# The byte places of matmul operands in a fp32r transformer layer: activations and slabs 128 bytes past the weight ring, one temporary in PSUM

## The chip, the core and the metric

The kernel runs on one core of one Trainium2 chip. The metric is the device time of one execution in microseconds. Before the change the median of three runs is 1975.04 us (1974.83 to 1975.86). A measurement is one launch; the profile is of one execution of its own.

## What is computed

One layer of a decoder: 512 tokens, width 2048, all in float32. A combined input projection feeds four mixers (pooling, convolution, two sparse attentions), then comes an output projection, a normalisation, a SwiGLU block and a second normalisation:

```python
D_MODEL, SEQ, DEPTH = 2048, 512, 1
D_FF = 5632
mix = jnp.concatenate([y_pool, y_conv, y_dsa, y_nsa], axis=-1)
x = _layernorm(DN_ALPHA * x + mix @ w_out[l], ln1_g[l], ln1_b[l])
gate, up = jnp.split(x @ w_gate_up[l], 2, axis=-1)
x = _layernorm(DN_ALPHA * x + (jax.nn.silu(gate) * up) @ w_down[l], ln2_g[l], ln2_b[l])
```

The part that the change is about is the last two lines, the feed-forward block, 1206 of the 1973 us of the span.

## The kernel before

**Three matmuls for one.** Every float32 operand is split into a high part (a cast to fp32r) and a low part (the operand less its high part). A product takes three fp32r matmuls: high by high, high by low, low by high. In the code a group of three lines is one such step: L795 to L797, L1030 to L1032, L1148 to L1152, L1197 to L1201, L1237 to L1239. Each `matmul` call is a load of 128 weight columns (the second argument, the stationary operand) and a matmul that streams the third argument, the moving operand. ScalarE makes the high parts (L1485), VectorE the low parts (L2034).

**The feed-forward block** is cut by a scheme of seven block products in place of eight (`PIECES = 7`). It runs in 62 units, one behind the other. 42 are chunks (`chunk`): 128 hidden features of gate and up, 7 products of 24 matmuls with 256 moving columns. In a chunk the ring of weight granules is the weights; what moves is `act` in products 1, 5, 6 and 7, and the block sums in `x_room` (products 2 and 3) and in `xs_4` (product 4, shown as `xs`). 20 are down units (`down`), two after every third chunk of four: 7 products of 12 matmuls with 512 moving columns. There the ring granule moves, and the weights are blocks of the hidden values: `h01` and `h23` (shown as `h`), `hs21` and `hs4` (shown as `hs`). After the last chunk a tail of 16 blocks of 12 long matmuls finishes the down product, on granules in `w_room` and, for every second pair, in `x_room` (`late`).

**Earlier products.** The input projection uses whole slabs in `w_hi` and `w_lo` (L795). The output projection (L1030) has `act` as weights and a slab as moving operand; the slab lies in `w_room` or, for a part, in `x_room`. The first gate and up slabs use `w_room` and `xs_4`.

**Places in SBUF.** Tensors stand one behind the other in a partition. `w_room` starts at byte 2240, 192 modulo 512. Ring granules are slices of it at multiples of 4096 bytes (`ring_hi`), or that plus 512 (`ring_lo`), so they are at 192. Slabs start `SHIFT` columns later: with `SHIFT = 8`, 32 bytes, at 224. `act`, `raw` and all tensors of the feed-forward stage up to `x_room` start at 224. Slabs and block sums in `x_room` start `SHIFT` columns into it, at 256; `xs_4` is at 256. The late granules start at the front of `x_room`, at 224. Columns of a slice step by multiples of 512 bytes, so a slice has its tensor's place.

**Order of work around the change.** Each engine's order is written out by hand and the engines meet at counting semaphores. In a chunk ScalarE copies intermediate sums out of PSUM, takes SiLU of the first half (L1579, `p5_temp`) and of the second (L1585, `g2_temp`); VectorE multiplies (L2134, h2). `g2_ready` and `h2_ready` count these. `temps` holds five temporaries of 256 columns, `g2_temp` the first. In a down unit ScalarE copies the first product, `d1` (banks 2 and 3), into `d2` (banks 0 and 1) at L1597, and TensorE's third product accumulates there behind `down_seeded`. PSUM banks 4 and 5 hold `r1`, bank 6 `r2`, bank 7 `r3`, each in its first 256 columns.

Of the kernel before, what the change touches and what calls it, by code (L numbers as in the profile page):

```python
# [21 lines left out]
F32 = mybir.dt.float32  # L22
F32R = mybir.dt.float32r
ALU = mybir.AluOpType
ACT = mybir.ActivationFunctionType
AX = mybir.AxisListType

P = 128
SEQ = 512
# [34 lines left out]
FF_CHUNKS = D_FF // P  # L64
# [34 lines left out]


GRAN = SLAB // 2
SHIFT = 8
HALF_TOKS = SEQ // 2
S_ORDER = ("s1", "s2", "s4", "s3")
TAIL_SLOTS = ((0, 32), (2, 32), (4, 63), (5, 63), (1, 32), (3, 32), (0, 33), (2, 33))
# [36 lines left out]
def build(nc, x, x_t, w_in, w_out, pool_w, pool_scale, conv_w, conv_b, conv_ln_g, conv_ln_b, conv_pw_w,  # L142
          conv_pw_b, cmp_pos_k, cmp_pos_v, cmp_k_w1, cmp_k_w2, cmp_v_w1, cmp_v_w2, ln1_g, ln1_b,
          ln2_g, ln2_b, w_gate_up, w_down, out):
    with ExitStack() as ctx:
        def sb(name, shape, dt=F32, where=ctx):
            return where.enter_context(nc.sbuf_tensor(name, shape, dt))
# [12 lines left out]
        act_hi, act_lo = act[:, 0, :, :], act[:, 1, :, :]  # L160
        raw = sb("raw", [P, 2, SLAB])

        mixing = ExitStack()
        with mixing:
            def sbm(name, shape):
# [34 lines left out]
        hs21 = sb("hs21", [P, 2, 2, SEQ], F32R, feed)  # L200
        stage = sb("stage", [P, 4, 2, SEQ], F32, feed)
        raw_c = sb("raw_c", [P, 2, GRAN], F32, feed)
        temps = sb("temps", [P, 5, HALF_TOKS], F32, feed)
        a12_scope = ExitStack()
        with a12_scope:
            a12 = sb("a12", [P, KT // 2, HALF_TOKS], F32, a12_scope)
# [80 lines left out]
                     "s3": act_lo[:, 0:kh, HALF_TOKS:SEQ]}  # L287
        s_source = {"s1": s1, "s2": a22, "s4": a12, "s3": a11}

        g2_temp, s_temp, p5_temp, p16_temp, p167_temp = (temps[:, i, :] for i in range(5))  # L290
        rstd_diagonal, ones_row = temps[:, 0, 0:P], temps[0:1, 0, P:2 * P]
        feed_ident, small = temps[:, 1, 0:P], temps[:, 1, P:2 * P]
        stats = small[:, 0:TT * 24].rearrange("p (i n s) -> p i n s", i=TT, n=4)
        moments = small[:, TT * 24:TT * 26].rearrange("p (i s) -> p i s", i=TT)
        rstd, shift = small[:, TT * 26:TT * 27], small[:, TT * 27:TT * 28]
        silu_g = temps[:, 3:5, :].rearrange("p a n -> p (a n)")
        r1 = [psum[:, 4 + i, 0:HALF_TOKS] for i in range(2)]
        r2, r3 = psum[:, 6, 0:HALF_TOKS], psum[:, 7, 0:HALF_TOKS]
        d1, d2, d3 = psum[:, 2:4, :], psum[:, 0:2, :], psum[:, 5:8:2, :]
# [492 lines left out]
        def _(pe):  # L792
# [457 lines left out]
            for e in range(16):  # L1250
                i, n = e // 4, e % 4
                if e < 2:
                    pe.wait_ge(x21_copied, N_DOWN)
                elif e < 4:
                    pe.wait_ge(x11_copied, N_DOWN)
                elif e >= 8:
                    pe.wait_ge(tile_added, added + e - 8 + 1)
                elif e == 4:
                    pe.wait_ge(c11_done, FF_CHUNKS - 2)
                    pe.wait_ge(g2_ready, FF_CHUNKS - 2)  # L1260
                    pe.wait_ge(c12_done, FF_CHUNKS - 1)
                for k in range(4):
                    piece = 2 * n + k // 2
                    if e == 0 and k == 0:
                        pe.wait_ge(hid_lo, hid_last - 2)
                    if k == 3 and n == 0 and i in (0, 2):
                        pe.wait_ge(hid_lo, hid_last - 1 + i // 2)
                    if i == 0 and piece < 4:
                        pe.wait_ge(lo_ready, TAIL_Q + piece + 1)
                    elif i == 0:  # L1270
                        pe.wait_ge(late_low, piece - 3)
                    w_h, w_l = late[piece - 4] if piece >= 4 else (ring_hi(TAIL_Q + piece), ring_lo(TAIL_Q + piece))
                    mm = down_products(i, k, e % 8, w_h, w_l, k % 2)
                mm.then_inc(tail_tile, 1)
# [16 lines left out]
        def _(act):  # L1291
# [232 lines left out]
            def chunk(un):  # L1524
                m, par, g = un.m, un.par, un.m // 4
                j, prev, kind = m % 2, (m - 1) % 2, m % 4
                last = g == FF_GROUPS - 1

                act.wait_ge(gran_done, un.q + 1)
                if m == 0:  # L1530
                    act.wait_ge(silu_done, 2)
                else:
                    act.wait_ge(g2_ready, m)
                nc.scalar.copy(r2, r1[par]).then_inc(p1_seeded, 1)
                unit_high(un, 4)
                if kind in (1, 2):
                    act.wait_ge(h2_ready, m)
                    part_high(h22, prev, p167_temp)
                elif m > 0:
                    act.wait_ge(h2_ready, m)  # L1540
                    part_high(h11, prev, nat[:, prev, 0:HALF_TOKS])

                act.wait_ge(gran_done, un.q + 2)
                if m > 0:
                    act.wait_ge(h1_ready, m)
                nc.scalar.copy(p5_temp, r3).then_inc(p5_copied, 1)
                unit_high(un, 5)
                if kind in (1, 2) and not last:
                    act.wait_ge(base_stored[1], 16)
                    act.wait_ge(s_nat, 6 * g + 2 * kind + 1)  # L1550
                    part_high(hs21, prev, nat[:, prev, :])
                    act.wait_ge(s_nat, 6 * g + 2 * kind + 2)
                    part_high(hs4, prev, s_temp)
                elif kind == 3 and g == FF_GROUPS - 2 or kind == 0 and last:
                    part_high(hs3, prev, nat[:, prev, HALF_TOKS:SEQ])
                elif kind in (0, 3) and m > 0:
                    act.wait_ge(s_nat, 6 * (g + (1 if kind == 3 else 0)) + prev + 1)
                    part_high(hs3, prev, s_temp)

                act.wait_ge(gran_done, un.q + 3)  # L1560
                if m == 0:
                    act.wait_ge(hid_ready, 2)
                elif kind in (1, 2):
                    act.wait_ge(hid_lo, low_count(m - 1, "a12"))
                nc.scalar.copy(p16_temp, r2).then_inc(p16_copied, 1)
                unit_high(un, 6)

                act.wait_ge(gran_done, un.q + 4)
                following(un, 0)

                act.wait_ge(gran_done, un.q + 5)
                if kind in (1, 2):
                    act.wait_ge(hid_lo, low_count(m - 1, "a22"))
                nc.scalar.copy(p167_temp, r2).then_inc(p167_copied, 1)
                following(un, 1)

                act.wait_ge(gran_done, un.q + 6)
                act.wait_ge(c22_ready, m + 1)
                nc.scalar.activation(p5_temp, r1[par], ACT.Silu).then_inc(c11_done, 1)  # L1579
                following(un, 2)  # L1580

                act.wait_ge(gran_done, un.q + 7)
                if m > 0:
                    act.wait_ge(h2_ready, m)
                nc.scalar.activation(g2_temp, r2, ACT.Silu).then_inc(g2_ready, 1)  # L1585
                if kind in (0, 1):
                    act.wait_ge(h1_ready, m + 1)
                    part_high(h12, j, p16_temp)
                following(un, 3)

            def down(un):
# [2 lines left out]
                act.wait_ge(gran_done, un.q + 1)  # L1594
                if k > 0:
                    act.wait_ge(x21_copied, k)
                nc.scalar.copy(d2, d1).then_inc(down_seeded, 1)  # L1597
                unit_high(un, 4)

# [88 lines left out]
        def _(ve):  # L1688
# [388 lines left out]
            def chunk(un):  # L2077
# [53 lines left out]
                ve.wait_ge(g2_ready, m + 1)  # L2131
                ve.wait_ge(c22_ready, m + 1)
                h2 = p167_temp if kind < 2 else nat[:, j, HALF_TOKS:SEQ]
                nc.vector.tensor_tensor(h2, p167_temp, g2_temp, ALU.mult).then_inc(h2_ready, 1)  # L2134

            def down(un):
                k = un.k
# [116 lines left out]
```

## Time and profile before

| | |
|---|---|
| median of 3 runs | 1975.04 us |
| profiled execution | 1974.57 us |
| its span | 1972.8 us |
| TensorE matmul, weight load | 1963.5 us, 1732.0 us |
| VectorE, ScalarE, GpSimd | 1412.7, 848.8, 504.1 us |
| DMA | 264.28 MB, mean 134 GB/s |

The span runs from the first to the last instruction; 1.8 us of the execution lie around it. Busy time of TensorE counts overlapping matmuls once and their ends are modelled, so the mean duration of a matmul in the profile (280 ns for 256 moving columns) is longer than the spacing at which they start. The spacing is read from a stretch that holds one kind alone, as its length over the count of matmuls in it. The counts (x98 and the like) that a view of stretches gives take in matmuls that run across an edge, one to three more than start in it; a product of a chunk is 24 matmuls, one of a down unit 12. The granted clock was the full one, 2.4 GHz, over the whole span (PEclk 9 is 90% or more; the profile gives a mean of 1.0).

### The profile page before, as it was taken

Reading aid. Unit: us, or ns where it says so; the run is one execution under the profiler, and the core shown is the slowest. Engines: PE = TensorE matmul, PEld = TensorE weight load, DVE = VectorE, ACT = ScalarE, POOL = GpSimd, SP = SyncE. Lnnn points to the kernel's source line nnn. Section 1 sums busy time; section 2 is a strip of 40 time slices with the busy share of each in tenths; the row PEclk is TensorE's granted clock in tenths of the full one; section 3 lists DMA queues with packets and bytes.
Section 4 is the critical chain, followed back from the end, with each engine's and each line's share of the span. In section 5 each row is a group of like instructions: output and inputs, shape, how many; then the busy total and the mean of one; then the engine's idle time right before and its main releaser. Section 6 shows DMA issues by size and latency. Waiting matters only on the chain.

```text
span 1972.8 us, 30224 instructions
## 1 busy us (share of the span) xinstructions
PE 1963.5 (100%) x12301; PEld 1732.0 (88%) x12301; DVE 1412.7 (72%) x1911; ACT 848.8 (43%) x1280; POOL 504.1 (26%) x343
## 2 busy tenths in 40 slices
PE   9999999999999999999999999999999999999999
PEld 7777888766888999998989999898998989999897
DVE  3079997263112988787878888788788878878776
ACT  3011000364000645555555555555555555555553
POOL 2555656244557310202011020201102020110200
PEclk9999999999999999999999999999999999999999
DMA  7433343500534433938466494755739376493972
GB/s 213 106 87 85 86 106 85 176 22 22 213 102 133 150 84 113 193 103 182 118 148 152 128 176 125 156 144 120 180 107 192 113 156 150 110 197 91 198 248 87
DMA packets 316429, 264.28 MB, mean 134 GB/s; under 512 B 12262, under 2 KB 258854, under 8 KB 313482
## 3 DMA queue, kind: packets, MB, share of 16 engines
q1 hardware_dynamic: 292026, 211.97, 37.4%
q0 software_dynamic: 23616, 46.15, 14.2%
q10 hardware_dynamic: 656, 4.33, 0.6%
q8 instruction: 93, 1.52, 0.3%
q14 instruction: 38, 0.31, 0.1%
HBM read 211.95 MB, written 50.33 MB: 133 GB/s over the span
## 4 chain that ended last, share of the span: by engine, by line
PE 98%; DVE 1%; DMA 1%; SPq 0%; ACT 0%; issue 0%; DVEq 0%
PE psum L1148 14%; PE psum L1150 14%; PE psum L1152 14%; PE psum L795 7%; PE psum L797 7%; PE psum L796 7%; PE psum L1199 7%; PE psum L1201 7%; PE psum L1197 7%; PE psum L1030 3%; PE psum L1031 3%; PE psum L1032 3%; PE psum L1009 1%; PE psum L946 1%; PE psum L937 1%; PE psum L997 1%
## 5 line engine op out<-in xcount | busy, mean ns | idle before, releaser
L2034 DVE TENSOR_TENSOR w_room<-raw,w_room 128x1024 fp32r<-128x1024 f32 x310 | 379.3, 1223 | 157.2 <-ACT w_room L1485 157.1
L1485 ACT CAST w_room<-raw 128x1024 fp32r<-128x1024 f32 x312 | 328.7, 1053 | 209.6 <-DVE raw L2045 67.0
L765 POOL DMA_DIRECT2D out<-stage x160 | 139.5, 1471 | 1028.4 <-DVE stage L2145 1007.6
L1148 PE MATMUL psum<-act,w_room 128*128 128x256 f32 x1344 | 375.8, 280 | 0.0
L1150 PE MATMUL psum<-act,w_room 128*128 128x256 f32 x1344 | 375.5, 279 | 0.0
L1152 PE MATMUL psum<-act,w_room 128*128 128x256 f32 x1344 | 375.3, 279 | 0.0
L1148 PEld LDWEIGHTS psum<-act,w_room 128*128 128x128 f32 x1344 | 252.7, 188 | 0.5
L1150 PEld LDWEIGHTS psum<-act,w_room 128*128 128x128 f32 x1344 | 252.6, 188 | 0.5
L1152 PEld LDWEIGHTS psum<-act,w_room 128*128 128x128 f32 x1344 | 252.8, 188 | 0.0
L795 PE MATMUL psum<-act,w_room 128*128 128x512 f32 (+2 forms) x608 | 232.0, 382 | 1.6 <-DVE act L1709 1.6
L797 PE MATMUL psum<-act,w_room 128*128 128x512 f32 (+2 forms) x608 | 229.9, 378 | 0.0
L796 PE MATMUL psum<-act,w_room 128*128 128x512 f32 (+2 forms) x608 | 229.9, 378 | 0.0
L673 POOL TENSOR_TENSOR w_room<-raw,w_room 128x2048 fp32r<-128x2048 f32 (+1 forms) x45 | 207.5, 4612 | 3.7
L2034 DVE TENSOR_TENSOR w_room<-raw_c,w_room 128x1024 fp32r<-128x1024 f32 x124 | 151.5, 1222 | 59.0 <-ACT w_room L1485 57.2
L1148 PE MATMUL psum<-x_room,w_room 128*128 128x256 f32 x672 | 185.6, 276 | 0.0
L1152 PE MATMUL psum<-x_room,w_room 128*128 128x256 f32 x672 | 185.5, 276 | 0.0
L1150 PE MATMUL psum<-x_room,w_room 128*128 128x256 f32 x672 | 185.5, 276 | 0.0
L670 POOL TENSOR_SCALAR w_room<-raw 128x2048 fp32r<-128x2048 f32 (+1 forms) x45 | 88.8, 1973 | 259.7 <-PE psum L797 136.6
L795 PEld LDWEIGHTS psum<-act,w_room 128*128 128x128 f32 (+1 forms) x608 | 113.8, 187 | 27.3 <-issue 5.1
L797 PEld LDWEIGHTS psum<-act,w_room 128*128 128x128 f32 (+1 forms) x608 | 113.8, 187 | 22.1
L796 PEld LDWEIGHTS psum<-act,w_room 128*128 128x128 f32 (+1 forms) x608 | 113.8, 187 | 22.0 <-issue 0.5
L1485 ACT CAST w_room<-raw_c 128x1024 fp32r<-128x1024 f32 x126 | 132.7, 1053 | 0.0
(303 smaller groups left out, 4131.9 us busy)
## 6 DMA issues: line engine op xcount, KB each, us to landing
raw_c<-in_w_gate_up SPq DMA_DIRECT2D x84, 512.0 KB, 6.6
raw<-in_w_gate_up SPq DMA_DIRECT2D x84, 512.0 KB, 5.6
out<-stage POOLq DMA_DIRECT2D x160, 256.0 KB, 8.2
raw<-in_w_in SPq DMA_DIRECT2D x30, 1024.0 KB, 5.8
raw<-in_w_down SPq DMA_DIRECT2D x46, 512.0 KB, 4.7
raw_c<-in_w_down SPq DMA_DIRECT2D x42, 512.0 KB, 3.8
raw<-in_w_out SPq DMA_DIRECT2D x16, 1024.0 KB, 5.1
acc<-in_x SPq DMA_DIRECT2D x1, 4096.0 KB, 12.4
```

What stands on the lines that cost most here:

```text
L673: nc.gpsimd.tensor_tensor(lo, raw[:, slot, 0:words], hi.bitcast(F32), ALU.subtract)\
L765: nc.gpsimd.dma_start(out_dram[:, tile, n * SEQ:(n + 1) * SEQ], part, accum_op=ALU.add)\
L795: nc.tensor.matmul(out_ap, stat_hi, mov_hi, start=first, stop=False)
L796: nc.tensor.matmul(out_ap, stat_hi, mov_lo, start=False, stop=False)
L797: return nc.tensor.matmul(out_ap, stat_lo, mov_hi, start=False, stop=last)
L1148: nc.tensor.matmul(out_ap, stat_hi[:, cols], mov_hi[:, k, :], start=opens and k == 0, stop=False, skip_group_check=not opens)
L1150: nc.tensor.matmul(out_ap, stat_hi[:, cols], mov_lo[:, k, :], start=False, stop=False, skip_group_check=not opens)
L1152: mm = nc.tensor.matmul(out_ap, stat_lo[:, cols], mov_hi[:, k, :], start=False, stop=k == kh - 1, skip_group_check=not opens)
L1197: nc.tensor.matmul(out_ap[:, i, :], room[:, 0, j, toks], w_h[:, cols], start=opens and j == 0, stop=False, skip_group_check=not opens)
L1199: nc.tensor.matmul(out_ap[:, i, :], room[:, 1, j, toks], w_h[:, cols], start=False, stop=False, skip_group_check=not opens)
L1485: nc.scalar.copy(ring_hi(at), src).then_inc(hi_ready, 1)
L2034: nc.vector.tensor_tensor(lo, src, hi.bitcast(F32), ALU.subtract).then_inc(lo_ready, 1)
```

## The change

It changes places in SBUF, moves one temporary to PSUM, and adds three kinds of waits. No instruction is added, removed or moved on any engine.

`SHIFT` goes from 8 to 32 columns, 128 bytes. `act` and `raw` now start at 320 modulo 512, slabs in `w_room` at 192 + 128 = 320. A spacer `between` of 384 bytes follows `raw`, so that the tensors of both stages behind it start at 192: `nat`, `hs4`, `hs21`, `stage`, `raw_c`, `temps`, `h01`, `h23`, `x_room`. The ring stays at 192. Slabs and block sums in `x_room` are at 320, `xs_4` at 320, late granules at 192.

The room for this comes from `temps`, four temporaries in place of five. The SiLU result g2 now lies in columns 256 to 511 of PSUM bank 1, and for the last chunk of bank 6. Bank 1 is a part of `d2`, so ScalarE's copy into `d2` waits for h2 in even down units, and TensorE's fifth tail block and the last use of `temps` wait for the last h2.

```diff
-SHIFT = 8
+SHIFT = 32
...
         raw = sb("raw", [P, 2, SLAB])
+
+        between = sb("between", [P, P - SHIFT])
...
-        temps = sb("temps", [P, 5, HALF_TOKS], F32, feed)
+        temps = sb("temps", [P, 4, HALF_TOKS], F32, feed)
...
-        g2_temp, s_temp, p5_temp, p16_temp, p167_temp = (temps[:, i, :] for i in range(5))
-        rstd_diagonal, ones_row = temps[:, 0, 0:P], temps[0:1, 0, P:2 * P]
-        feed_ident, small = temps[:, 1, 0:P], temps[:, 1, P:2 * P]
+        s_temp, p5_temp, p16_temp, p167_temp = (temps[:, i, :] for i in range(4))
+        g2_room = [psum[:, bank, HALF_TOKS:SEQ] for bank in (1, 6)]
+        rstd_diagonal, ones_row = temps[:, 1, 0:P], temps[0:1, 1, P:2 * P]
+        feed_ident, small = temps[:, 0, 0:P], temps[:, 0, P:2 * P]
...
-        silu_g = temps[:, 3:5, :].rearrange("p a n -> p (a n)")
+        silu_g = temps[:, 2:4, :].rearrange("p a n -> p (a n)")
...
                     pe.wait_ge(c12_done, FF_CHUNKS - 1)
+                    pe.wait_ge(h2_ready, FF_CHUNKS - 2)
...
-                nc.scalar.activation(g2_temp, r2, ACT.Silu).then_inc(g2_ready, 1)
+                nc.scalar.activation(g2_room[m == FF_CHUNKS - 3], r2, ACT.Silu).then_inc(g2_ready, 1)
...
                     act.wait_ge(x21_copied, k)
+                if k % 2 == 0:
+                    act.wait_ge(h2_ready, 4 * (k // 2) + 3)
                 nc.scalar.copy(d2, d1).then_inc(down_seeded, 1)
...
-                nc.vector.tensor_tensor(h2, p167_temp, g2_temp, ALU.mult).then_inc(h2_ready, 1)
+                nc.vector.tensor_tensor(h2, p167_temp, g2_room[m == FF_CHUNKS - 3], ALU.mult).then_inc(h2_ready, 1)
```

## Rows read from the trace of the kernel before

**Rows 1.** The page: busy time by engine, and the granted clock in 40 slices.

```profile
PE 1963.5 (100%) x12301; PEld 1732.0 (88%) x12301; DVE 1412.7 (72%) x1911; ACT 848.8 (43%) x1280; POOL 504.1 (26%) x343
PEclk9999999999999999999999999999999999999999
```

**Rows 2.** Waits of TensorE, the longest group: us in total, times, longest.

```profile
PE psum L795 <- DVE act L1709: 1.6, 2, 1.3
```

**Rows 3.** Stretches (from:to, us, busy us with counts, clock, DMA): a chunk; all units.

```profile
859.27:878.64 19.37, 19.37 (x170) 19.37 (x169) 17.32 (x24) 10.75 (x18) 0.00 (x0) 1.00 0.38 113
710.66:1916.97 1206.31, 1206.31 (x8737) 1129.93 (x8736) 986.20 (x1114) 674.86 (x915) 142.20 (x166) 1.00 0.62 148
```

**Rows 4.** Groups of TensorE by line and shape: busy us, mean ns, idle before.

```profile
L1148 PE MATMUL psum<-act,w_room 128*128 128x256 f32 x1344 | 375.8, 280 | 0.0
L1148 PE MATMUL psum<-x_room,w_room 128*128 128x256 f32 x672 | 185.6, 276 | 0.0
...
L1197 PE MATMUL psum<-w_room,h 128*128 128x512 f32 x320 | 126.5, 395 | 0.0
L1197 PE MATMUL psum<-w_room,hs 128*128 128x512 f32 x240 | 94.9, 396 | 0.0
...
L1148 PE MATMUL psum<-xs,w_room 128*128 128x256 f32 x336 | 92.8, 276 | 0.0
...
L1030 PE MATMUL psum<-x_room,act 128*128 128x512 f32 x32 | 12.7, 398 | 0.0
```

**Rows 5.** Stretches of 256 columns: `act`, 4 products; block sums, 3; gate slab.

```profile
838.95:850.16 11.21, 11.21 (x96) 11.17 (x96) 0.00 (x0) 0.00 (x0) 1.00 0.22 63
...
850.16:858.33 8.17, 8.17 (x75) 8.17 (x74) 4.83 (x4) 3.17 (x3) 0.00 (x0) 1.00 0.50 147
666.94:669.82 2.88, 2.88 (x26) 2.88 (x25) 0.00 (x0) 0.00 (x0) 0.00 (x0) 1.00 1.12 306
```

**Rows 6.** Stretches of 512 columns: down products on h; tail block on x_room and h.

```profile
780.61:791.81 11.20, 11.20 (x48) 8.83 (x47) 0.00 (x0) 0.00 (x0) 1.00 0.63 119
...
1922.57:1928.04 5.47, 5.47 (x24) 4.32 (x23) 2.79 (x3) 0.00 (x0) 0.00 (x0) 1.00 0.06 24
```

**Rows 7.** The same: up slabs in xs_4 and in w_room; x_room against act.

```profile
688.13:699.32 11.19, 11.19 (x48) 8.83 (x48) 0.00 (x0) 0.00 (x0) 0.00 (x0) 1.00 0.19 54
...
699.32:710.21 10.89, 10.89 (x48) 8.82 (x47) 2.44 (x2) 1.05 (x1) 0.00 (x0) 1.00 0.17 42
...
624.63:630.25 5.62, 5.60 (x24) 4.31 (x23) 0.00 (x0) 0.00 (x0) 0.00 (x0) 1.00 0.63 168
```

**Rows 8.** The stretch of the 32 matmuls of L982 (32 moving columns, 128 weight columns).

```profile
404.11:407.60 3.49, 3.49 (x32) 3.49 (x31) 1.00 0.02 5
```

**Rows 9.** Groups of ScalarE and VectorE by line and shape.

```profile
L1585 ACT ACTIVATE temps<-psum 128x256 f32<-128x256 f32 x42 | 16.2, 385 | 17.1 <-PE psum L1152 17.1
...
L1534 ACT COPY psum<-psum 128x256 f32<-128x256 f32 x42 | 15.0, 357 | 42.1 <-PE psum L1152 42.1
...
L2110 DVE TENSOR_TENSOR temps<-psum,temps 128x256 f32<-128x256 f32 x42 | 17.5, 416 | 0.3 <-PE psum L1152 0.2
...
L2134 DVE TENSOR_TENSOR temps<-temps 128x256 f32<-128x256 f32 x22 | 9.2, 418 | 0.0
```

**Rows 10.** Timeline around the first down unit: start us, us, engine, line.

```profile
761.01 0.28 PE L1148 MATMUL psum<-act,w_room 128*128 128x256 f32 x1
...
775.01 0.40 PE L1197 MATMUL psum<-w_room,hs 128*128 128x512 f32 x1
...
772.41 1.00 ACT L1597 COPY psum<-psum 128x1024 f32<-128x1024 f32 x1 [1.47 <-PE psum L1201]
...
772.92 0.42 DVE L2134 TENSOR_TENSOR nat<-temps 128x256 f32<-128x256 f32 x1
```

**Rows 11.** Stretches of the first chunk: act products; block sums in x_room.

```profile
721.95:733.47 11.52, 11.52 (x96) 11.47 (x96) 0.00 (x0) 0.00 (x0) 1.00 0.44 117
...
713.47:719.12 5.65, 5.65 (x48) 5.61 (x48) 0.00 (x0) 0.00 (x0) 0.00 (x0) 1.00 0.33 95
```

## The prediction

> **What bounds the kernel now.** I read the page first: TensorE is busy for 1963.5 of 1972.8 us at the full granted clock [rows 1]. Its waits come next, and the longest group is 1.6 us [rows 2]. So the time is the sum of the spacings of the matmuls, and nothing can shorten it except the spacing itself. The page's mean durations (280 ns for 256 moving columns) do not show that spacing, because matmuls overlap. I took it from stretches that hold one kind of matmul: length of the stretch over the count in it. The stretches of the feed-forward part, 1206.31 us of the span [rows 3], are the ones that the change is about, and the counts of its kinds are in [rows 4].
>
> Each matmul reads a moving operand and, for the next one, 128 weight columns (512 bytes a partition). Call d the place of the moving operand less that of the weights, in bytes modulo 512. All slices start at multiples of 512 bytes, so d is one number for a kind. Before the change it is +32 for `act` against the ring, +64 for `x_room` and `xs_4` against it, and -32 in the down products, where the ring moves and an h block is the weights. The spacings:
>
> 256 moving columns: d = +32, 11.21 us for 96, 116.8 ns; d = +64, 8.17 us for 72, 113.5 ns; d = 0, 2.88 us for 24, 120.0 ns [rows 5].
> 512 moving columns: d = -32 (ring against h), 11.20 us for 48, 233.3 ns; d = 0 (late slabs in `x_room` against h), 5.47 us for 24, 227.9 ns, the latter with one change of kind in it [rows 6]. The gate and up slabs say the same: `xs_4` against `act`, d = -32, 11.19 us for 48, 233.1 ns, and right behind it `w_room` against `act`, d = 0, 10.89 us for 48, 226.9 ns. `x_room` against `act`, d = +32, is at 5.62 us for 24, 234.2 ns [rows 7].
>
> The columns alone would take 256/2.4 = 106.7 and 512/2.4 = 213.3 ns, so the excess is 6.8 to 13.3 ns in the short kind and 13.6 to 20 in the long. It follows d, with shape, engine and clock unchanged.
>
> Here a rule of the Trainium skill speaks against the change. TensorE: Matmul & The Clock Gate, section Part 2: What happens when you issue a matmul, says that TensorE has two independent SBUF read ports and that loading the next weights takes no read bandwidth from the running matmul. By that rule alone a place modulo 512 is worth nothing and the time would stay at 1975.0; the spacings of [rows 5 to 7] disagree with it, since two kinds that differ in d alone are 6 ns apart.
>
> **The change part by part.** After it, d is 0 in every product with 512 columns and +128 in every feed-forward product with 256.
>
> Down products, d from -32 to 0. 960 + 720 = 1680 matmuls (the first and the hs kind of L1197 stand for three lines each, [rows 4]) x (233.3 - 226.9) = 10.8 us. This term is measured at both ends. In the tail the 96 matmuls on `w_room` and h get the same, 0.6 us; the output projection's 96 on `x_room` lose 234.2 - 226.9, 0.7 us (L1030, L1031, L1032, 32 each), and the up slab's 48 on `xs_4` lose 6.2, 0.3 us [rows 4, 6, 7]. Together 1.6 us. Every product with 512 columns that was at d = 0 stays there, and so do the 192 short ones of the gate slabs.
>
> Chunk products, d from +32 and +64 to +128. No row has a short matmul at +128, so this is bounded from both sides. From below by the columns, 106.7 ns; the nearest real row is 32 short matmuls at L982 whose period is set by the loading of 128 weight columns: 3.49 us for 32, 109.1 ns [rows 8]. From above, without a new mechanism, by the best place seen, 113.5 ns. The three places fall by 3.2 and 3.3 ns for each 32 bytes: 120.0, 116.8, 113.5. One more such step gives 110.2, two would pass the 109.1 of L982. I take 110.0, the next step, near the row of L982. Then 4032 matmuls (1344 x 3) on `act` x 6.8 = 27.4 us, and (672 + 336) x 3 = 3024 on the slabs x 3.5 = 10.6 us [rows 4, 5]. Bounds: at 113.5 the two are 13.3 and 0; at 109.1, 31.0 and 13.3; at 106.7, 40.7 and 20.6.
>
> The Trainium skill (same page, section Back-to-back issue gap) has N/2.4 + 2.5 ns for a matmul at the full clock, 109.2 ns at 256 columns. An estimate by that page alone would put the kernel at about 1919 us; the 109.1 of L982 agrees with the size, and no matmul of 256 columns in this trace reaches it.
>
> The g2 temporary in PSUM. ScalarE's SiLU writes 256 columns in 385 ns to SBUF, its copies to PSUM of the same size take 357; VectorE's product with a PSUM operand takes 416 ns against 418 [rows 9]. 42 of each, under TensorE's work: nothing on the path. Both banks are idle then, except for d2.
>
> That exception is the added wait. In every even down unit (10 of 20) ScalarE's copy of d1 into d2 (L1597) now waits for VectorE's h2. In the first of them the copy starts at 772.41 with 1.00 us to run, h2 ends at 772.92 + 0.42 = 773.34, and TensorE, which opened the down unit 24 long matmuls earlier (5.6 us, 769.4), opens its third product at 775.01 [rows 10]. The copy moves 0.95 us later and ends near 774.4, 0.6 us before TensorE asks. Behind it on ScalarE stand the next ring cast and the copy of d3, which TensorE needs one product (2.8 us) later; that absorbs it. But a quicker TensorE eats the cover: h2's chain starts at the end of the fourth product of the chunk (761.01 in that row, then low part, difference, cast, low part, without a rest over 0.5 us), and from there to 775.01 TensorE runs 72 short matmuls and 24 long ones. At 110.0 and 226.9 these shrink by 72 x 6.8 + 24 x 6.4 = 0.64 us, all of the cover. I put 0.5 us for the ten; at 109.1 it is 1.3, at 106.7 3 us, at 113.5 none. The wait added ahead of the fifth tail block is for the last h2, and four blocks of 12 long matmuls (11 us) lie between the last chunk and it; h2 ends some 4 us after a chunk (773.34 against 769.4), so it costs nothing.
>
> VectorE next. A chunk lasts 19.37 us with 17.3 us of VectorE work in it [rows 3]. 168 x 110.0 = 18.5 us still holds it. The waits that it has come from ScalarE's casts, which start when TensorE ends a product, and its results are asked for several products later.
>
> Sum: 27.4 + 10.6 + 10.8 + 1.6 - 0.5 = 49.9 us off the profiled execution's 1974.57 gives 1924.7. The median of the runs is 0.5 us above that execution, so 1925.
>
> **Rivals.** (a) The place stops mattering past 64 bytes: all short matmuls at 113.5. For it: the excess there, 6.8 ns, may be a floor that has nothing to do with places; at d = +64 the spacing is even, which looks like a settled state. Against: L982's 109.1 and the even steps. Gain 13.3 + 10.8 + 1.6 = 25.7, time 1949.5.
>
> (b) Short matmuls fall into a slow rhythm at +128, slower than before. The trace has two rhythms at one place: in the first chunk `act` at d = +32 runs at 11.52 us for 96, 120.0 ns, and `x_room` at +64 at 5.65 for 48, 117.7, though later both run at 116.8 and 113.5 [rows 5, 11]. And the long kind is not even in d: it is best at 0 and 6 ns worse on either side [rows 6, 7]. If +128 settled at 120.0: 4032 x 3.2 + 3024 x 6.5 = 32.6 lost, 12.4 gained, time 1995. It decides from a mean short spacing of 115.3 (19.37/168) + 12.4/7056 = 117.1 ns.
>
> (c) No effect of places, the two-ports rule: 1975. The rows are against it.
>
> (d) The short spacing goes to the columns' 106.7: 40.7 + 20.6 + 12.4 - 3 = 70.7, time 1904. VectorE would then have 17.3 us of work in a 17.9 us chunk and the wait for h2 would show.
>
> **How the numbers follow.** Forecast (109 to 112 ns) 0.56, time 1918 to 1940; (a) with its surroundings up to 115 ns 0.27; (b) 0.10, 0.07 of it past 117.1; gains eaten by something unseen, so that little or nothing is left, and (c) 0.04; (d) 0.03. A measurement of this kernel tells 0.2%, 4 us, from no change. The range of 8 in 10 takes in 109.1 with no stall, 1918, less a little for faster, and (a) with 2 us on top: 1914 to 1952. Faster 0.56 + 0.27 + 0.03 and 0.03 of (b), 0.89; same 0.04; slower 0.07.
>
> **What would show it.** In a stretch of `act` products 96 matmuls in 10.56 us, and the slabs' spacing equal to that of `act`, since d is now the same; in a down unit 48 in 10.89. A chunk of 18.5 us. If `act` and the slabs agree at 113.5, it is (a); if the down products stay at 233.3, the place of h was not the cause and 10.8 us fall away; a wait of TensorE for ScalarE at the third product of even down units, ten times, under 0.1 us each, shows the added wait. A steady spacing above 117.1 makes the forecast wrong in sign.

## The result, and the profile after

The changed kernel takes 1996.4 us (median of 4 runs, 1996.0 to 1996.5) against 1974.9 for the kernel before beside it (4 runs, 1973.7 to 1975.9). The ratio is 1.0106, interval 1.0094 to 1.0118: slower, by 21.4 us. The forecast was 1925, range 1914 to 1952. The time is that of rival (b), 1995.

The page of the changed kernel; these lines answer to [rows 1].

```profile
span 1994.2 us, 30226 instructions
...
PE 1984.1 (99%) x12301; PEld 1764.0 (88%) x12301; DVE 1414.4 (71%) x1911; ACT 846.3 (42%) x1280; POOL 503.8 (25%) x343
...
PEclk9999999999999999999999999999999999999999
```

TensorE's busy time grew by 20.6 us, with the same 12301 matmuls at the same granted clock, and the span by 21.4. The other engines' busy times are within 2.5 us of before. The waits of TensorE in the changed kernel (us in total, times, longest), which answer to [rows 2]:

```profile
PE psum L798 <- DVE act L1715: 2.2, 3, 1.1
PE psum L805 <- POOL ident L655: 1.5, 1, 1.5
PE psum L1000 <- ACT pt L1424: 0.9, 2, 0.7
```

The first three groups are shown. No wait of TensorE lies in the feed-forward part, and the longest group, which lies ahead of it, is 2.2 us where it was 1.6. So the loss is in the spacing. Stretches of the changed kernel that hold one kind (from:to, us, busy us with counts by engine, clock, DMA), against [rows 5, 6] and, for the whole chunk in the last line, [rows 3]:

```profile
821.03:832.55 11.52, 11.52 (x98) 11.52 (x97) 10.09 (x12) 5.22 (x7) 0.00 (x0) 1.00 0.64 165
832.55:838.31 5.76, 5.76 (x50) 5.76 (x49) 3.69 (x6) 3.25 (x6) 0.00 (x0) 1.00 0.58 168
838.31:841.19 2.88, 2.88 (x26) 2.88 (x25) 1.56 (x3) 1.32 (x2) 0.00 (x0) 1.00 0.69 193
782.31:793.19 10.88, 10.88 (x49) 9.01 (x49) 10.30 (x10) 5.75 (x6) 5.38 (x7) 1.00 0.68 138
821.03:841.19 20.16, 20.16 (x170) 20.16 (x169) 15.34 (x19) 9.79 (x15) 0.00 (x0) 1.00 0.63 170
```

In order: `act`, 96 matmuls in 11.52 us, 120.0 ns, where it was 116.8; block sums in `x_room`, 48 in 5.76, 120.0, where it was 113.5; `xs_4`, 24 in 2.88, 120.0; 48 down products in 10.88, 226.7, where it was 233.3; a chunk, 20.16 us for 19.37. The sum closes: 4032 x 3.2 + 3024 x 6.5 = 32.6 us lost, 12.4 gained, 20.2 in all, of 21.4 measured; the other 1.2 is inside the interval of the ratio (18.6 to 23.3 us). It lies ahead of the feed-forward part, which opens at 710.9 us, 0.3 later than before, though the prediction had gained 1.0 us there; 0.6 us of that went into the longer first wait.

The groups of TensorE say the same in their way: the mean durations of the three lines rise on `act` from 279 or 280 to 281, 284 and 285 ns, on `x_room` from 276 to as much as 285, and fall on h from 395 to 389. They answer to [rows 4].

```profile
L1155 PE MATMUL psum<-act,w_room 128*128 128x256 f32 x1344 | 383.0, 285 | 0.0
L1153 PE MATMUL psum<-act,w_room 128*128 128x256 f32 x1344 | 381.7, 284 | 0.0
L1151 PE MATMUL psum<-act,w_room 128*128 128x256 f32 x1344 | 377.7, 281 | 0.0
...
L1155 PE MATMUL psum<-x_room,w_room 128*128 128x256 f32 x672 | 191.5, 285 | 0.0
...
L1200 PE MATMUL psum<-w_room,h 128*128 128x512 f32 x320 | 124.5, 389 | 0.0
```

The added wait is there, and TensorE does not pay for it: no wait of its own is listed in this part. Timeline of the changed kernel around the first down unit (start us, us, engine, line, [idle before]), which answers to [rows 10]:

```profile
774.70 0.41 DVE L2140 TENSOR_TENSOR nat<-temps,psum 128x256 f32<-128x256 f32 x1
775.20 1.00 ACT L1603 COPY psum<-psum 128x1024 f32<-128x1024 f32 x1 [2.25 <-DVE nat L2140]
776.11 1.05 ACT L1489 CAST w_room<-raw 128x1024 fp32r<-128x1024 f32 x1
776.91 0.39 PE L1200 MATMUL psum<-w_room,hs 128*128 128x512 f32 x1
```

ScalarE's copy into d2 stands 2.25 us for h2 (22.7 us in the ten even down units), ends at 776.20, and TensorE opens the third product at 776.91. The prediction had 0.6 us of cover there; with slower short matmuls it is 0.7.

### The profile page after: what moved, and what is told of

Read it like the earlier page. It is cut to its first block, busy times and chain, and to the rows that moved or that the text cites. A ratio compares the mean times of both kernels' runs of the same rounds, so it can differ in the third digit from the quotient of the medians.

```text
span 1994.2 us, 30226 instructions
## 1 busy us (share of the span) xinstructions
PE 1984.1 (99%) x12301; PEld 1764.0 (88%) x12301; DVE 1414.4 (71%) x1911; ACT 846.3 (42%) x1280; POOL 503.8 (25%) x343
## 4 chain that ended last, share of the span: by engine, by line
PE 98%; DVE 1%; DMA 1%; SPq 0%; ACT 0%; issue 0%; DVEq 0%
PE psum L1155 14%; PE psum L1153 14%; PE psum L1151 14%; PE psum L798 7%; PE psum L800 7%; PE psum L799 7%; PE psum L1202 6%; PE psum L1204 6%; PE psum L1200 6%; PE psum L1033 3%; PE psum L1035 3%; PE psum L1034 3%; PE psum L1012 1%; PE psum L949 1%; PE psum L940 1%; PE psum L1000 1%
## 5 line engine op out<-in xcount | busy, mean ns | idle before, releaser
L1155 PE MATMUL psum<-act,w_room 128*128 128x256 f32 x1344 | 383.0, 285 | 0.0
L1153 PE MATMUL psum<-act,w_room 128*128 128x256 f32 x1344 | 381.7, 284 | 0.0
L1151 PE MATMUL psum<-act,w_room 128*128 128x256 f32 x1344 | 377.7, 281 | 0.0
L1151 PEld LDWEIGHTS psum<-act,w_room 128*128 128x128 f32 x1344 | 255.3, 190 | 0.4
L1155 PEld LDWEIGHTS psum<-act,w_room 128*128 128x128 f32 x1344 | 254.0, 189 | 0.0
L1153 PEld LDWEIGHTS psum<-act,w_room 128*128 128x128 f32 x1344 | 252.7, 188 | 0.4
L1155 PE MATMUL psum<-x_room,w_room 128*128 128x256 f32 x672 | 191.5, 285 | 0.0
L1153 PE MATMUL psum<-x_room,w_room 128*128 128x256 f32 x672 | 190.8, 284 | 0.0
L1151 PE MATMUL psum<-x_room,w_room 128*128 128x256 f32 x672 | 188.8, 281 | 0.0
```

Of the source, the lines that this page charges most:

```text
L1151: nc.tensor.matmul(out_ap, stat_hi[:, cols], mov_hi[:, k, :], start=opens and k == 0, stop=False, skip_group_check=not opens)
L1153: nc.tensor.matmul(out_ap, stat_hi[:, cols], mov_lo[:, k, :], start=False, stop=False, skip_group_check=not opens)
L1155: mm = nc.tensor.matmul(out_ap, stat_lo[:, cols], mov_hi[:, k, :], start=False, stop=k == kh - 1, skip_group_check=not opens)
```

## The experiments

All kernels below are the changed kernel, g2 in PSUM and the added waits included, with other places. `raw` moves with `act`, and the other tensors behind `between` (`temps`, `nat`, `stage` and the like) move with the h blocks. The ring stands still in all of them. "Rhythm" is the spacing that a kind keeps over whole products, where one place shows more than one. Places are given less that of the ring, in bytes modulo 512, in the order `act` (and `raw`) / slabs and block sums in `x_room` / `xs_4` / h blocks; the kernel before is at 32 / 64 / 64 / 32, the changed one at 128 / 128 / 128 / 0. A diff is against the changed kernel; `SLAB_SHIFT` stands where `SHIFT` stood in the three uses for `x_room`, and `between` sets h, with (h - `act`) / 4 columns modulo 128. In the table the spacings (ns) are from the chunks after the first pair of down units; "before" is the median of the kernel before, run beside it on the same chip; n is the number of runs.

| kernel | places | act | x_room | xs_4 | long, h | us (n) | before |
|---|---|---|---|---|---|---|---|
| changed | 128/128/128/0 | 120.0 | 120.0 | 120.0 | 226.7 | 1996.38 (4) | 1974.93 |
| g2_only | 32/64/64/32 | 116.8 | 113.4 | 113.3 | 233.3 | 1975.53 (10) | 1975.26 |
| h_only | 32/64/64/0 | 116.8 | 113.4 | 113.3 | 226.7 | 1964.43 (4) | 1975.26 |
| shift16 | 64/64/64/0 | 117.8 | 117.8 | 117.8 | 226.7 | 1978.61 (10) | 1975.26 |
| shift24 | 96/96/96/0 | 120.0 | 120.0 | 120.0 | 226.7 | 1995.62 (1) | 1975.26 |
| shift48 | 192/192/192/0 | 117.8 | 117.8 | 117.8 | 226.7 | 1979.14 (10) | 1975.06 |
| shift64 | 256/256/256/0 | 120.0 | 120.0 | 120.0 | 226.7 | 1994.55 (1) | 1975.06 |
| plus128 | 160/192/192/0 | 117.3 | 113.7 | 113.3 | 226.7 | 1964.71 (1) | 1974.45 |
| minus | 480/448/448/0 | 118.3 | 114.0 | 113.3 | 226.7 | 1969.45 (1) | 1975.06 |
| act128_slab64 | 128/64/64/0 | 118.7 | 117.8 | 117.8 | 226.7 | 1983.59 (1) | 1974.45 |
| act32_slab128 | 32/128/128/0 | 116.7 | 118.5 | 118.7 | 226.7 | 1980.75 (1) | 1974.45 |
| act64_slab32 | 64/32/32/0 | 117.8 | 116.6 | 116.7 | 226.7 | 1974.32 (1) | 1975.69 |
| all64_h32 | 64/64/64/32 | 117.8 | 117.8 | 117.8 | 233.3 | 1990.16 (1) | 1974.45 |
| h_64 | 32/64/64/64 | 117.6 | 114.6 | 114.5 | 233.3 | 1982.13 (1) | 1975.69 |
| xs4_96 | 64/64/96/0 | 117.8 | 117.8 | 120.0 | 226.7 | 1982.40 (1) | 1975.06 |
| xs4_32 | 64/64/32/0 | 117.8 | 117.8 | 116.6 | 226.7 | 1977.26 (11) | 1975.69 |
| xs4_160 | 192/192/160/0 | 113.7 | 113.3 | 117.2 | 226.7 | 1960.16 (1) | 1975.69 |
| xs4_160b | the same | 113.7 | 113.3 | 117.2 | 226.7 | 1957.13 (5) | 1974.67 |
| s1_160 | 192/160, 192/192/0 | 113.3 | 116.0 | 113.3 | 226.7 | 1955.76 (4) | 1974.67 |

(h_64: mean over the whole program for the short kinds, since its rhythm changes from chunk to chunk. act32_slab128: 116.7 is what `act` takes in two of three stretches; the first one behind each pair of down units is at 117.8. Single runs of a kernel scatter by some 2 us, as the ranges of the repeated ones show.)

**The change in parts: g2_only and h_only.** Both take the place of the slabs from `SLAB_SHIFT`. The first keeps the old places and has only g2 in PSUM and the waits, the second also moves the h blocks and nothing else.

```diff
-SHIFT = 32
+SHIFT = 8
+SLAB_SHIFT = 8        # h_only: 16, and between of 120 columns
...
-        between = sb("between", [P, P - SHIFT])
```

> The changed kernel with every place as in the kernel before (SHIFT 8, no spacer; act and h 32 bytes past the ring, slabs 64): only g2 in PSUM and its waits are left of the change. Three theories. Place: the spacing of the 256-column matmuls follows d, the place of the moving operand past the ring, so here they are back at 116.8 ns on act and 113.4 on the slabs and the time is 1975 within 3 us. Rhythm: the spacing of the long matmuls before them (now d = 0) carries over; here the long ones are at 233.3 again, so 1975 too. Waits: g2 in PSUM or the added waits make the short matmuls slow; then 1994 to 1998 and a spacing of 120.0.

Measured: ratio 1.0004 (0.9995 to 1.0014). Its `act` and `x_room` run as before the change, at 116.8 and 113.5 ns:

```profile
818.71:829.92 11.21, 11.21 (x98) 11.21 (x98) 9.88 (x13) 5.24 (x7) 0.00 (x0) 1.00 0.68 172
829.92:835.37 5.45, 5.45 (x50) 5.45 (x49) 3.85 (x5) 3.25 (x6) 0.00 (x0) 1.00 0.48 139
```

g2 in PSUM and its waits cost nothing that these ten runs can tell.

> The changed kernel with act 32 and slabs 64 bytes past the ring, as before the change, and the h blocks at the ring's place: of the places only those of the 512-column products are changed. Place: long matmuls at 226.9 ns, short ones as before the change, 1975 - 11 = 1964, 1961 to 1966. Rhythm: long ones at 226.9 and the short ones at 120.0 all the same: 1995. Waits: as place or slower than 1975 if the waits are at fault.

Measured: ratio 0.9945 (0.9928 to 0.9961), 10.8 us off. Its stretches, `act`, `x_room`, then the same two in the first chunk, then down products on h:

```profile
821.81:833.02 11.21, 11.21 (x98) 11.21 (x98) 9.88 (x13) 5.24 (x7) 0.00 (x0) 1.00 0.68 172
833.02:838.47 5.45, 5.45 (x50) 5.45 (x50) 3.85 (x5) 3.25 (x6) 0.00 (x0) 1.00 0.50 141
725.29:736.80 11.51, 11.51 (x98) 11.51 (x97) 9.86 (x13) 5.54 (x8) 0.00 (x0) 1.00 0.45 121
716.80:722.46 5.66, 5.66 (x50) 5.66 (x50) 5.66 (x7) 4.07 (x6) 0.00 (x0) 1.00 0.33 95
783.65:794.53 10.88, 10.88 (x49) 9.02 (x49) 10.30 (x10) 5.75 (x6) 5.36 (x7) 1.00 0.68 137
```

48 long matmuls in 10.88 us, 226.7 ns, with the short ones at 116.8 and 113.4 as before. What the changed kernel loses against this one, 32 us, comes from the places of `act` (with `raw`) and of the slabs. Lines three and four are the slow rhythm that the first chunk had before too [rows 11].

**The curve of places: shift16, shift24, shift48, shift64.** `act` and slabs together, h at 0.

```diff
-SHIFT = 32
+SHIFT = 16            # shift24: 24, shift48: 48, shift64: 64
+SLAB_SHIFT = 16       # the same number
-        between = sb("between", [P, P - SHIFT])
+        between = sb("between", [P, 112])        # 128 - SHIFT
```

> The changed kernel with act and slabs 64 bytes past the ring (SHIFT 16), h blocks at its place. Place: all short matmuls at 113.4 ns, long at 226.9: 1975 - 13.5 - 12 = 1949, 1946 to 1953. Rhythm: short ones at 120.0, 1996.

> The changed kernel with act and slabs 96 bytes past the ring (SHIFT 24), h blocks at its place: the point between 64 (113.4 ns before the change) and 128 (120.0 after it). Place: if the fall of 3.3 ns per 32 bytes goes on one step and breaks off behind it, 110.2 ns and 1926; if the spacing has its lowest point at 64 and is symmetric about it, as 32 bytes on the other side, 116.8 ns and 1973; if it breaks off past 64, 120.0 and 1996. Rhythm: 120.0 and 1996.

Both expectations were off for shift16: at one place for all, 64 gives neither 113.5 nor 120.0 but 117.8 (ratio 1.0016, 1.0007 to 1.0026). Stretches of shift16, `act` and `x_room`:

```profile
817.88:829.18 11.30, 11.30 (x98) 11.30 (x97) 9.87 (x12) 5.23 (x7) 0.00 (x0) 1.00 0.61 176
829.18:834.84 5.66, 5.66 (x50) 5.66 (x49) 3.86 (x6) 3.25 (x6) 0.00 (x0) 1.00 0.54 158
```

The block sums stand at the very place that gave 113.4 in h_only, and take 117.8, the value of the first chunk of the kernel before. So the place of an operand alone does not fix its spacing. shift24, at 96, is as slow as the changed kernel; of its expectations the one that the fall breaks off past 64 came.

> The changed kernel with act and slabs 192 bytes past the ring (SHIFT 48), h at its place. In plus128 the slabs at 192 ran at 113.4 ns from the first chunk on, with act at 160. Place (192 has one rhythm, 113.3): all short matmuls at 113.4, long at 226.9: 1949, 1946 to 1952. Rhythm by change of place alone (as shift16 at 64, where a uniform place stayed at 117.8): 117.8 to 120, 1979 to 1996.

> The same at 256 bytes past the ring. Period 128, as after (128) and the gate slabs (0) suggest, both 120.0: 120.0 and 1996. Symmetric about 192 with period 512: no row; between 1949 and 1996. Nearest row, 192: 1949.

shift48 is shift16 again (117.8, ratio 1.0018, 1.0008 to 1.0028), shift64 the changed kernel (120.0). The `act` stretches of shift24 and of shift64:

```profile
820.62:832.14 11.52, 11.52 (x98) 11.52 (x97) 10.09 (x12) 5.22 (x7) 0.00 (x0) 1.00 0.64 166
...
819.89:831.41 11.52, 11.52 (x99) 11.52 (x98) 10.09 (x12) 5.22 (x7) 0.00 (x0) 1.00 0.59 150
```

Where all short kinds stand at one place, 128 and 256 give 120.0, as 96 does, and 64 and 192 give 117.8. At 0 there is the gate slab of [rows 5] alone, 120.0 in every run, wherever `act` and the slab stood together. These points repeat after 128 bytes.

**The old pair of places elsewhere: plus128 and minus.**

```diff
-SHIFT = 32
+SHIFT = 40            # minus: 120
+SLAB_SHIFT = 48       # minus: 112
```

> h_only (1964.4 us) with act and slabs 128 bytes further: act 160, slabs 192 bytes past the ring, h at its place. Period 128: only the place modulo 128 counts for the short matmuls, which is why 128 runs like 0 (both 120.0); then it is h_only again, act 116.8, slabs 113.4, 1964 within 3. Period 512 or 256: a place of its own, and the nearest ones measured, 96 and 128, are at 120.0: 1995.

> act 32 and slabs 64 bytes ahead of the ring (480 and 448 modulo 512), h at its place. Mirror: only the distance counts, then act 116.8 and slabs 113.4 and 1964. Sign counts: the long matmuls lost as much on either side (233.3), the short ones may not; at 120.0 for both it is 1996.

plus128 keeps all of the gain of h_only (1964.71 against 1964.43), as its first expectation had it. Its `act` and `x_room`:

```profile
817.21:828.48 11.27, 11.27 (x98) 11.27 (x98) 9.93 (x13) 5.24 (x7) 0.00 (x0) 1.00 0.67 172
828.48:833.93 5.45, 5.45 (x50) 5.45 (x49) 3.78 (x5) 3.25 (x6) 0.00 (x0) 1.00 0.53 147
```

minus, the mirror image, lies between its two expectations: 5 us slower than h_only, nearly all of it in `act` (118.3), with slabs close to the quick value. Moving `act` and slabs by 128 bytes is thus not bad in itself. What the changed kernel did was to put all of them at +128, one of the places (96, 128, 256) that run at 120.0.

**One of the two moved: act128_slab64, act32_slab128, act64_slab32.**

```diff
+SLAB_SHIFT = 16       # act128_slab64, SHIFT stays 32, between of 96
...
+SHIFT = 8             # act32_slab128, SLAB_SHIFT = 32, between of 120
...
+SHIFT = 16            # act64_slab32, SLAB_SHIFT = 8, between of 112
```

> h_only with act alone moved from 32 to 128 bytes past the ring; slabs stay at 64. Place: each kind goes by its own place, act at 120.0 adds 4032 x 3.2 = 12.9: 1977. Rhythm, that is, the spacing at one place depends on what ran before (shift16 ran all of it at 117.8 at the place where h_only has 113.4): act at 120.0 and the slabs at 113.4 or 117.8, the latter adds 13.3 more: 1990.

> h_only with the slabs alone moved from 64 to 128 bytes past the ring; act stays at 32. Place: slabs at 120.0 add 3024 x 6.6 = 20: 1984. Rhythm: act, too, leaves 116.8 for the 120.0 that it has in the first chunk of the kernel before, 12.9 more: 1997.

Stretches of `act` and `x_room`, first two of act128_slab64, then two of act32_slab128 a chunk further on:

```profile
819.88:831.28 11.40, 11.40 (x98) 11.40 (x97) 9.97 (x12) 5.23 (x7) 0.00 (x0) 1.00 0.64 169
831.28:836.93 5.65, 5.65 (x50) 5.65 (x49) 3.77 (x6) 3.25 (x6) 0.00 (x0) 1.00 0.56 161
...
840.55:851.76 11.21, 11.21 (x98) 11.21 (x98) 9.74 (x13) 5.55 (x8) 0.00 (x0) 1.00 0.20 56
851.76:857.44 5.68, 5.68 (x50) 5.68 (x50) 5.44 (x9) 3.88 (x7) 0.00 (x0) 1.00 0.50 142
```

`act` at 128 between slabs at 64 takes 118.7, not 120.0, and these slabs 117.8; slabs at 128 behind `act` at 32 take 118.5, not 120.0. So a kind's neighbours count, and both expectations missed for both kernels (1977 or 1990 against 1983.59, 1984 or 1997 against 1980.75).

> h_only with the two places exchanged: act at 64, slabs at 32. Rhythm entered from 32: act 4032 at 113.4, slabs 3024 at 116.8: 1964.4 - 13.7 + 10.3 = 1961. Otherwise act at 117.8: 1979.

Stretches of act64_slab32, `act` in the first chunk and after the first pair of down units:

```profile
720.66:731.55 10.89, 10.89 (x98) 10.89 (x97) 9.21 (x11) 5.54 (x8) 0.00 (x0) 1.00 0.42 120
816.77:828.08 11.31, 11.31 (x98) 11.31 (x97) 9.90 (x13) 5.22 (x7) 0.00 (x0) 1.00 0.61 173
```

One kernel, one operand, one place: 96 matmuls in 10.89 us and later in 11.31. These are the two rhythms at 64, 113.4 and 117.8. The quick one came behind slabs at 32 and was gone behind long matmuls, so the time lies between the two expectations (1961 and 1979).

**Do the long matmuls set it? all64_h32 and h_64.**

```diff
+SHIFT = 16            # all64_h32: SLAB_SHIFT = 8, between of 120
...
+SHIFT = 8             # h_64: SLAB_SHIFT = 0, between of 8
```

> shift16 (1978.6, all short matmuls at 117.8) with the h blocks back at 32 bytes past the ring, so that the long matmuls before the chunks run at d = -32 as in the kernel before. Rhythm set by the long matmuls: short ones fall to 113.4, long ones 233.3: 1978.6 - 31 + 11 = 1959. Rhythm set by the change of place among the short ones (none here): they stay at 117.8: 1990. Place alone can't explain shift16.

> h_only (1964.4) with the h blocks at 64 past the ring, so the long matmuls run at d = -64. Cost grows with distance: over 233.3, 1976 or more. As at 32: 233.3, 1975. Cost by distance modulo 64: 226.9, 1964. The short ones keep 116.8 and 113.4 in each case.

all64_h32 gives 117.8 with long matmuls at 233.3, as shift16 with 226.7: with all short kinds at 64 the long kind's own pace does not set theirs. Its `act`:

```profile
819.06:830.36 11.30, 11.30 (x99) 11.30 (x98) 9.86 (x12) 5.23 (x7) 0.00 (x0) 1.00 0.57 167
```

In h_64 the place of h, which no short matmul reads, does change the short ones: whole stretches take the slow rhythm, and the 1982.13 is above its expectation for 233.3 (1975). Stretches of h_64: down products on h, `x_room` right behind them, `act` in two successive chunks:

```profile
781.28:792.48 11.20, 11.20 (x49) 9.02 (x48) 10.54 (x10) 6.03 (x6) 5.72 (x7) 1.00 0.68 127
812.08:817.74 5.66, 5.66 (x50) 5.66 (x49) 4.40 (x6) 3.25 (x6) 1.14 (x2) 1.00 1.12 198
820.56:832.08 11.52, 11.52 (x98) 11.52 (x97) 10.08 (x12) 5.24 (x7) 0.00 (x0) 1.00 0.55 162
840.25:851.46 11.21, 11.21 (x99) 11.21 (x97) 9.87 (x13) 5.55 (x8) 0.00 (x0) 1.00 0.22 64
```

The slabs are at 117.8, then `act` takes 120.0 and a chunk later 116.8 at one place; it is so behind every pair of down units. The down products with h at 64 are at 233.3, as with h at 32.

**A change of place to enter the quick rhythm: xs4_96, xs4_32, xs4_160, xs4_160b, s1_160.** One slab alone stands elsewhere.

```diff
+SHIFT = 16            # xs4_32, xs4_96; 48 in xs4_160, xs4_160b, s1_160
+SLAB_SHIFT = 16       # the same number
+            below_s4 = sb("below_s4", [P, 120], F32, s4_scope)   # xs4_96: 8
...
-            below_s1 = sb("below_s1", [P, SHIFT], F32, a2_scope)     # s1_160 alone
+            below_s1 = sb("below_s1", [P, SLAB_SHIFT - 8], F32, a2_scope)
```

> shift16 (all short matmuls 64 bytes past the ring, a uniform 117.8, 1978.6 us) with one change: the block sums in xs_4, one product of seven in a chunk, at 96. Rhythm by change of place: each return from 96 to 64 can tip act and x_room into the 113.4 that the slabs have at 64 in the kernel before; then 6048 x 4.4 = 26.6 off, 1952 to 1957. Place alone: the six stay at 117.8, xs_4 goes to 118 to 120, 1979 to 1982.

> shift16 (act and slabs at 64, uniform 117.8, 1978.6 us) with xs_4, one product of seven, at 32. Rhythm entered from 32: from the first chunk's fourth product on act and x_room run at 113.4 and xs_4 at 116.8: 5040 x 4.4... counted as 4032 + 2016 = 6048 x 4.4 = 26.6 and 1008 x 1.0: 1951, within 3. Rhythm tipped only by alternating in every second product, or lost in the down units: between 1951 and 1978. Place alone: 117.8 stays, 1977 to 1979.

xs4_96 stays in the slow rhythm: coming from 96 to 64 does not help. xs4_32 ended level with before (ratio 1.0008, 0.9999 to 1.0017), 26 us above what the quick rhythm throughout would give (1951). Its `act` and `x_room` in the first chunk, and after the first pair of down units:

```profile
722.16:733.04 10.88, 10.88 (x98) 10.88 (x98) 9.29 (x11) 5.54 (x8) 0.00 (x0) 1.00 0.41 120
733.04:738.48 5.44, 5.44 (x51) 5.44 (x50) 5.37 (x9) 3.98 (x7) 0.00 (x0) 1.00 0.39 108
...
818.03:829.33 11.30, 11.30 (x99) 11.30 (x98) 9.89 (x12) 5.23 (x7) 0.00 (x0) 1.00 0.59 173
829.33:834.99 5.66, 5.66 (x51) 5.66 (x50) 3.86 (x6) 3.25 (x6) 0.00 (x0) 1.00 0.57 162
```

It runs quick until the first down units and in no chunk behind them.

> shift48 (act and slabs at 192, uniform 117.8) with xs_4 at 160. Only the place modulo 128 counts: the same as xs4_32, whichever that is. In plus128 the slabs at 192 were at 113.4 after act at 160, so by the rhythm 1951.

> xs4_160 once more: 1960.2, 1959 to 1962, if the rhythm is the same in every execution. If it is chance, single executions between 1951 and 1978.

The same arrangement 128 bytes further comes back to the quick rhythm after every pair of down units. It was expected to do as xs4_32 did, and it did not. Stretches of xs4_160b right behind the first pair: `act` 24, `x_room` 48, `xs_4` 24, `act` 96, `x_room` 48:

```profile
805.56:808.38 2.82, 2.82 (x25) 2.78 (x24) 2.82 (x4) 2.74 (x3) 2.51 (x4) 1.00 1.11 148
808.38:814.04 5.66, 5.66 (x50) 5.66 (x49) 4.56 (x6) 3.41 (x7) 1.38 (x2) 1.00 1.12 194
814.04:816.89 2.85, 2.85 (x26) 2.85 (x25) 1.58 (x3) 1.32 (x2) 0.00 (x0) 1.00 1.11 252
816.89:827.77 10.88, 10.88 (x98) 10.88 (x97) 9.44 (x12) 5.24 (x7) 0.00 (x0) 1.00 0.63 167
827.77:833.21 5.44, 5.44 (x50) 5.44 (x50) 4.17 (x6) 3.31 (x6) 0.00 (x0) 1.00 0.46 129
```

117.8, 117.8 and 118.9 up to the end of `xs_4`; then 113.4 and 113.3. The step from `xs_4` at 160 to `act` at 192 is where it turns. Ratio 0.9913 (0.9899 to 0.9926). The traces of xs4_160 and xs4_160b have the same short spacings, so the rhythm is not chance; the median, 1957.13, is 3 us below the single run of xs4_160 on another chip, and just outside the 1959 to 1962 expected.

> xs4_160 with the entering product moved: of the block sums only s1 (second product of a chunk) lies at 160, act, s2 and xs_4 at 192, h at the ring's place. Entered by a step from 160 to 192, kept at 192: in each of the 11 chunks behind long matmuls product 1 stays at 117.8, product 2 at about 119, products 3 and 4 come to 113.4 from 117.8 and 119, 24 x (4.4 + 5.6) less 24 x 1 = 0.2 us each, 2.4 in all; every other chunk has one product at 117.3 either way: 1958, and x_room and xs at about 115 and 113.4. If entering depends on more than the step (as xs4_32 lost it after the first down units, where xs4_160 did not), act and xs stay at 117.8 and it is 1978.

Here the odd slab is s1, half of the block sums in `x_room`. Stretches of s1_160: `act` behind the down units, then `act`, `x_room` and `xs_4` a chunk on:

```profile
805.30:808.13 2.83, 2.83 (x25) 2.79 (x25) 2.83 (x4) 2.75 (x3) 2.51 (x4) 1.00 1.22 172
816.43:827.31 10.88, 10.88 (x98) 10.88 (x97) 9.55 (x13) 5.24 (x7) 0.00 (x0) 1.00 0.68 177
827.31:832.87 5.56, 5.56 (x50) 5.56 (x49) 4.20 (x7) 3.31 (x6) 0.00 (x0) 1.00 0.47 133
832.87:835.60 2.73, 2.73 (x26) 2.73 (x26) 1.54 (x3) 1.32 (x2) 0.00 (x0) 1.00 0.75 216
```

The step to the quick rhythm now lies at the third product of a chunk, so the slow stretch behind down units is shorter. 1955.76 us (1954.20 to 1957.28), ratio 0.9905 (0.989 to 0.992): faster than both kernels, 18.9 us below the one before. By spacings and counts: 4032 x 3.2 - 2016 x 2.5 + 12.4 = 20.3 (3.2 is 116.8 less 113.6, the mean of `act` over the program; 12.4 is the prediction's figure for the 512-column products); the spans of the two profiled executions, 1972.8 and 1952.4, are 20.4 apart. The ranges of s1_160 and xs4_160b overlap, so which of the two is faster is open.

## Why the prediction was wrong

The step that failed is the one for the chunk products: "I take 110.0, the next step". It drew a line through 120.0, 116.8 and 113.5 ns at d = 0, +32 and +64 and went on to +128; and the bound from above, 113.5, was the best value seen, not the worst. The measured spacing there is 120.0, so the terms of 27.4 and 10.6 us gained were 12.9 and 19.7 lost, 70.6 us between them, nearly all of the error (1996.4 less 1925 is 71.4).

Two things were wrong with that line. First, where all short kinds stand at one place the spacing repeats after 128 bytes (shift16 and shift48, changed and shift64), so +128 takes the value of 0, and the trace had it: 120.0, the gate slab of [rows 5]. I took the place modulo 512, the size of a weight row, and had no row for that choice. Second, 113.5 at +64 is not that place's value but one of two, and in the kernel before it stands behind products at +32. With all at +64 it is 117.8 (shift16). The 116.8 at +32 is no single value either: it is the mean of a cycle of four spacings (last section). So the three points of the line were not of one kind. The trace of before showed that in its first chunk [rows 11], and rival (b) quoted these rows; it got a chance of 0.10, with no reason given why a new place should not do what the first chunk did. Its arithmetic, 32.6 lost and 12.4 gained, is what came.

Right by their own steps were: the down products, "1680 matmuls x (233.3 - 226.9) = 10.8", which run at 226.7 in h_only, a kernel 10.8 us faster as a whole, its tail included; g2 in PSUM at nothing, 1.0004 alone. Not put to the test: the bound from VectorE, since chunks grew longer, and the 0.5 us for the added wait with a TensorE at 110 ns; at 120 no wait is seen. In s1_160, at 113.3, none is listed either, but some spacings around the third product of nine of the ten even down units are 233 to 237 ns in place of 226.7, 0.25 us in all; the changed kernel and h_only have none of these. That fits an added wait that begins to show, for which the prediction had nothing at 113.5; that it is the wait is not shown. The rule that speaks for rival (c) (the Trainium skill, TensorE: Matmul & The Clock Gate, section Part 2: What happens when you issue a matmul, two independent read ports) was rightly set aside as a forecast: h_only and the changed kernel run the same instructions and differ by 32 us. Whether the ports themselves are behind it no run shows. Rival (a), 113.5 past 64 bytes, is refuted by 120.0 at 96, 128 and 256. Rival (d) has no sign in any run.

What stays open: which part of TensorE's reading makes the two rhythms, and what tips them. Entering 64 from 32 does it in g2_only and h_only, though not at the first product of the first chunk, nor right behind the down units of h_64 (its slabs at 117.8 there); from 96 and from 128 not (xs4_96, act128_slab64); but minus, whose `act` at 480 is 96 modulo 128, has quick slabs, and xs4_32 loses for good what xs4_160 regains each time. So the tipping is not a function of places modulo 128 alone, or it depends on something that moved with them. No run tells these apart. The traces do show one regularity, at places 32 and 64: wherever a product at 32 ran at 120.0, the next one at 64 was quick (16 of 16 times: once each in before, g2_only, h_only, act64_slab32 and xs4_32, eleven times in h_64), while behind 116.7 at 32 both rhythms are seen. And since the ring never moved, no run tells the place past the ring from the place itself, except at 0, where the gate slabs stay at 120.0 wherever they and `act` stand.

## What to carry to other kernels

When TensorE is never idle and every matmul loads its own weights, read the spacing by kind from stretches of one kind, and sweep the operands' places against the weights in steps of 32 bytes over at least 128 before believing any line through three points. A spacing that appears with two values at one place in the trace, even in one early chunk, is a state that the neighbouring products set: it is a rival of full weight, and a value from a mixed sequence must not be used for a uniform one. Moving one slab 32 bytes off can pay more than aligning everything: 1957.13 and 1955.76 us with one slab at 160, 1979.14 with all at 192.

## What the runs showed of the hardware

With a new load of 128 weight columns for each matmul, at the full granted clock, the settled spacing of 256 moving columns was between 113.3 and 120.0 ns, most often 113.3, 116.7, 117.8 or 120.0, and of 512 columns 226.7 or 233.3, by places alone. (Places that alternate gave other values in between, as the table shows.) In periods of the 2.4 GHz clock those are 272, 280, 283 and 288, and 544 and 560: 16 to 32 and 32 to 48 above the columns. No run came below 113.3 in a product of 256 columns or below 226.6 in one of 512. The Trainium skill (the same page, section Back-to-back issue gap) has N/2.4 + 2.5 for an isolated matmul, that is 109.2 at 256 and 215.8 at 512; this case's stream, with a weight load for each matmul, stays above both. The 109.1 of [rows 8] is a matmul of 32 columns.

The same mean can hide a pattern. In the changed kernel the 120.0 repeats in threes: from one start to the next 117 or 118, 120 and 122 or 123 ns over the three matmuls of a step, the lines L1151, L1153 and L1155. The 116.8 of `act` in the kernel before repeats in fours: 120, 113, 116 and 117. Its 120.0 in the first chunk is even, and so, at 112 to 115, is the quick rhythm in s1_160.

The place of h, which no short matmul reads, changed the rhythm of later short ones (h_64 against h_only, behind down units: `act` at 120.0 in one chunk and 116.8 in the next, against 116.8 in both). A rhythm outlives what set it: in xs4_32 the slow one, entered in the first long matmuls, stayed for the rest of the program.
